# Seven products for eight in the HGRN projection of heads 2 to 7, and another order of the last normalisation

## The chip, the core and the metric

The kernel is one program on one core of a Trainium2 chip. Its engines are TensorE (PE in the profile, with its weight loads as PEld), VectorE (DVE), ScalarE (ACT), GpSimd (POOL) and SyncE (SP, which issues DMAs). Each has a queue of its own and runs it in order; they meet at semaphores. The metric is the time of one execution on the device in microseconds (us). On-chip memory is SBUF; TensorE writes to PSUM, here to two tensors: `prod_ps` (four banks of 128 x 512, for the products with weights) and `side_ps` (two pairs of banks of 128 x 1024, for everything else).

## What is computed

A hidden state of 1024 tokens with 1024 features passes a block with an HGRN2 mixer and an MLP, then a block with a convolution and retention mixer and an MLP, and is normalised once more at the end. All is float32.

```python
def _hgrn2_mixer(h, w_in, lower_bound, out_norm, w_out):
    q, f, i, g = jnp.split(h @ w_in, 4, axis=-1)
    k = (1.0 - lb) * jax.nn.sigmoid(-ff)
    qf = jax.nn.silu(q.astype(jnp.float32)) * (HGRN_HEAD_DIM ** -0.5)
    o = _hgrn2_chunk_scan(heads(qf), heads(k), heads(i.astype(jnp.float32)), heads(log_f))
    o = o * lax.rsqrt(jnp.mean(o * o, axis=-1, keepdims=True) + NORM_EPS)
    o = o.reshape(b, s, D_MODEL) * out_norm.astype(jnp.float32) * jax.nn.silu(g.astype(jnp.float32))
    return o.astype(h.dtype) @ w_out
# chunk scan, with decays from f: S_t = diag(f_t) S_{t-1} + k_t v_t^T ; o_t = S_t^T q_t, 8 heads of 128
# block 1: x = x + mix(rmsnorm(x)); x = x + squared_relu_mlp(rmsnorm(x)); rmsnorm(x). Block 2:
    h = h + hybrid_mixer(rms_norm(h, norm1_g), w_in, conv_w, conv_norm_g, ret_norm_g, w_out)
    h = h + sq_relu_mlp(rms_norm(h, norm2_g), w_up, w_down)
    return rms_norm(h, final_norm_g)
```

## The kernel before

**Units and products.** Weights come as a stream of units; one is a block of 128 output columns by 1024 inputs (`w_raw`, two slots). Each weight and each activation is split into a rounded high part and the rest (`w_hi`, `w_lo`; `operand_hi`, `operand_lo`), and a product of two such numbers takes three matmuls: high by high, high by low, low by high. So `product(u, slot, half, ...)` is 8 input tiles x 3 = 24 matmuls of 128 x 512 over one half of the tokens, and a unit has two halves. In what follows a "product" that is counted is one of these matmuls. A step named as `mid` stands behind the 12th. GpSimd splits a unit in `split_unit` (the high part at L710, the low at L714).

**The HGRN stage.** Head n has three units: v, f (which becomes the decay and the key k) and q. `hgrn_iteration(n)` stands once for each engine and holds three generations: the products of head n; the newer head n - 1, whose scores are computed in levels L0 to L6 (level L is the part of the chunk triangle at distance 2^L); and the older head n - 2, with the turning of v (`v`), the last level `L7`, the turning of k (`k`), the chunk sums (`kv`), the output (`o`) and its turning back (`back`). On TensorE these 13 side steps stand between the products, in `HG_ORDER`. They write the two pairs of `side_ps` in turn: a step waits in `pair_free` until the engine that reads the step two ahead of it has released the pair (`side_taken`). After how many products of head n each stands: v and L7 12, L0 24, k 36, L1 48, kv and L2 60, L3 84, o and L4 96, L5 120, L6 132, back 144.

For each level VectorE (`level`) multiplies the queries and keys by a decay that grows (L1932, for L1 the sigmoids in `hgrn_f`), renews the decay (L1933), and takes the scores from PSUM with a mask (L1954). From the product of VectorE, ScalarE gathers the weights for the next level on TensorE (`gather`, L2900 and L2901, tile `hgrn_mixed`). So a level needs VectorE's take of the level before and ScalarE's gather. Between levels VectorE scales the products (`group`, L1980), makes the keys (L2064, L2065), the norm factor of the older head (L1890 to L1895), its normalisation (L1900), the product of q with its sigmoid (L1990), and the states from kv (L2017, L2021). ScalarE takes v, k, o (L2925 and L2926) and back out of PSUM and makes the sigmoids (L2952, L2953 for f). Heads 4 to 7 are a loop of two heads on TensorE, VectorE and ScalarE.

**The paired form.** The in-projection of the second block, from its unit 6 on, is computed in eleven pairs of units. Over input tiles 0 to 3 the two units and the two token halves are a product of 2 x 2 blocks, for which seven block products are enough instead of eight; they need sums of weight blocks (S1 to S4, GpSimd in `split_paired`, high parts by ScalarE) and of activation blocks (T1 to T4, made once). A block product over two tiles is 2 x 3 = 6 matmuls. Input tiles 4 to 7 are computed in the plain way. ScalarE copies four partial results from PSUM to `in_c` (L3392); VectorE adds them to the banks (`got`: L1788, and L1798 for two buffers in SBUF).

**The end.** The last product's results are added to `x_res` piece by piece. Their squares are summed to the last normalisation (`end_last_sums`, L1244 on TensorE), each of three parts of the tokens gets its root, and `finals` (L2770 to L2778) multiplies on VectorE. SyncE stores.

## Time and profile before

| | us |
|---|---|
| median of three executions | 2270.77 |
| lowest, highest | 2270.21, 2271.34 |
| profiled execution, its own time | 2271.12 |
| profiled execution, span | 2269.2 |
| TensorE busy | 2256.1 (99%) |
| VectorE busy | 1637.3 (72%) |
| GpSimd busy | 1201.2 (53%) |
| ScalarE busy | 898.4 (40%) |

The span runs from the first to the last record of the profile; the execution's own time is 1.9 us more. Busy time is a sum over the whole program. In a timeline, what stands in brackets behind an instruction is how long its engine was idle ahead of it and which instruction ended that. Matmuls overlap in the records: a product of 0.39 us starts 0.23 us behind the one ahead, so their distance counts and not their length.

### The profile page before, as it was taken

Reading aid. Unit: us, or ns where it says so; the run is one execution under the profiler, and the core shown is the slowest. Engines: PE = TensorE matmul, PEld = TensorE weight load, DVE = VectorE, ACT = ScalarE, POOL = GpSimd, SP = SyncE. Lnnn points to the kernel's source line nnn. Section 1 sums busy time; section 2 is a strip of 40 time slices with the busy share of each in tenths; the row PEclk is TensorE's granted clock in tenths of the full one; section 3 lists DMA queues with packets and bytes.
Section 4 is the critical chain, followed back from the end, with each engine's and each line's share of the span. In section 5 each row is a group of like instructions: output and inputs, shape, how many; then the busy total and the mean of one; then the engine's idle time right before and its main releaser. Section 6 shows DMA issues by size and latency. Waiting matters only on the chain.

```text
span 2269.2 us, 32497 instructions
## 1 busy us (share of the span) xinstructions
PE 2256.1 (99%) x10794; PEld 1888.3 (83%) x10794; DVE 1637.3 (72%) x2305; ACT 898.4 (40%) x1467; POOL 1201.2 (53%) x1357
## 2 busy tenths in 40 slices
PE   9999999999999999999999999999999999999998
PEld 7888888888888888888888888888888888888887
DVE  7666666856778777876666777765787787778766
ACT  5233333324535434443432224322453454344433
POOL 4332323234566566656546665764556665666562
PEclk9999999999999999999999999999999999999999
DMA  4111010124264456455313111112335644554553
GB/s 158 38 29 37 29 37 28 38 75 148 93 214 148 176 185 201 145 190 186 112 56 121 66 38 40 53 56 102 121 134 182 213 148 176 185 203 146 186 196 138
DMA packets 59722, 273.82 MB, mean 121 GB/s; under 512 B 7152, under 2 KB 10352, under 8 KB 41712
## 3 DMA queue, kind: packets, MB, share of 16 engines
q1 hardware_dynamic: 59056, 270.51, 34.7%
q10 hardware_dynamic: 576, 2.13, 0.3%
q8 instruction: 54, 0.88, 0.2%
q14 instruction: 36, 0.29, 0.0%
HBM read 210.75 MB, written 61.87 MB: 120 GB/s over the span
## 4 chain that ended last, share of the span: by engine, by line
PE 94%; DVE 2%; DVEq 1%; ACT 1%; POOL 0%; DMA 0%; issue 0%; SPq 0%; ACTq 0%; POOLq 0%
PE prod_ps L959 10%; PE prod_ps L961 10%; PE prod_ps L960 10%; PE prod_ps L1225 8%; PE prod_ps L1227 8%; PE prod_ps L1226 8%; PE side_ps L1225 7%; PE side_ps L1226 7%; PE side_ps L1227 7%; PE side_ps L1100 2%; PE side_ps L1012 2%; PE prod_ps L1648 2%; PE prod_ps L1650 2%; PE prod_ps L1649 2%; PE prod_ps L1636 2%; PE prod_ps L1638 2%
## 5 line engine op out<-in xcount | busy, mean ns | idle before, releaser
L959 PE MATMUL prod_ps<-operand_hi,w_hi 128*128 128x512 f32 x984 | 393.1, 400 | 2.0 <-DVE operand_lo L1825 1.5
L961 PE MATMUL prod_ps<-operand_hi,w_lo 128*128 128x512 f32 x984 | 385.0, 391 | 0.0
L960 PE MATMUL prod_ps<-operand_lo,w_hi 128*128 128x512 f32 x984 | 383.9, 390 | 0.0
L710 POOL CAST w_hi<-w_raw 128x1024 fp32r<-128x1024 f32 x59 | 64.4, 1091 | 467.1 <-PE prod_ps L961 409.2
L755 POOL TENSOR_TENSOR w_lo<-w_raw,w_hi 128x256 fp32r<-128x256 f32 x168 | 155.6, 946 | 127.9 <-ACT w_hi L3049 127.1
L714 POOL TENSOR_TENSOR w_lo<-w_raw,w_hi 128x256 fp32r<-128x256 f32 x236 | 217.2, 951 | 4.7
L961 PEld LDWEIGHTS prod_ps<-operand_hi,w_lo 128*128 128x128 f32 x984 | 185.1, 188 | 40.1
L959 PEld LDWEIGHTS prod_ps<-operand_hi,w_hi 128*128 128x128 f32 x984 | 185.3, 188 | 38.6 <-DVE operand_lo L1825 1.9
L960 PEld LDWEIGHTS prod_ps<-operand_lo,w_hi 128*128 128x128 f32 x984 | 185.5, 188 | 36.0
L755 POOL TENSOR_TENSOR w_lo<-w_s,w_hi 128x256 fp32r<-128x256 f32 x168 | 129.1, 771 | 142.1 <-ACT w_more_hi L3057 115.9
L2257 DVE TENSOR_TENSOR x_res<-prod_ps,x_res 128x512 f32<-128x512 f32 x130 | 89.0, 685 | 96.2 <-PE prod_ps L1227 96.2
L3049 ACT ACTIVATE w_hi<-w_raw 128x512 fp32r<-128x512 f32 x114 | 70.9, 628 | 189.1 <-PE side_ps L1227 78.7
L2257 DVE TENSOR_TENSOR x_res<-side_ps,x_res 128x512 f32<-128x512 f32 x182 | 122.5, 684 | 27.4 <-PE side_ps L1227 23.3
L3053 ACT ACTIVATE w_hi<-w_s 128x512 fp32r<-128x512 f32 x114 | 72.0, 632 | 161.5 <-DVE w_s L2141 161.5
L755 POOL TENSOR_TENSOR w_s_lo<-w_s,w_more_hi 128x256 fp32r<-128x256 f32 x168 | 123.6, 756 | 0.0
L2242 DVE TENSOR_TENSOR wino_lo<-wino,wino_hi 128x1024 fp32r<-128x1024 f32 x78 | 110.3, 1426 | 11.3 <-ACT wino_hi L3120 9.2
L3057 ACT ACTIVATE w_more_hi<-w_s 128x512 fp32r<-128x512 f32 x114 | 71.9, 633 | 86.6 <-DVE w_s L2151 86.6
L1932 DVE TENSOR_TENSOR hgrn_kq<-hgrn_kq,hgrn_decay 128x1024 f32<-128x1024 f32 x48 | 59.3, 1235 | 51.2 <-PE side_ps L1100 49.6
L2900 ACT ACTIVATE hgrn_mixed<-hgrn_kq 128x256 f32<-128x256 f32 x56 | 23.8, 426 | 170.5 <-DVE hgrn_kq L1932 126.1
L755 POOL TENSOR_TENSOR w_a_lo<-w_raw,w_more_hi 128x256 fp32r<-128x256 f32 x84 | 68.4, 814 | 38.0 <-ACT w_more_hi L3060 38.0
L2141 DVE TENSOR_TENSOR w_s<-w_s,w_raw 128x256 f32<-128x256 f32 x114 | 77.3, 678 | 8.5
L3120 ACT ACTIVATE wino_hi<-wino 128x1024 fp32r<-128x1024 f32 x78 | 80.9, 1055 | 4.5 <-DVE wino L2246 2.7
(450 smaller groups left out, 6335.7 us busy)
## 6 DMA issues: line engine op xcount, KB each, us to landing
w_raw<-stream SPq DMA_DIRECT2D x202, 512.0 KB, 3.7
x_park<-x_res SPq DMA_DIRECT2D x45, 1024.0 KB, 8.2
x_res<-x_park SPq DMA_DIRECT2D x45, 1024.0 KB, 6.6
swapped<-op_park SPq DMA_DIRECT2D x39, 1024.0 KB, 5.0
op_park<-swapped SPq DMA_DIRECT2D x6, 1024.0 KB, 8.3
x_in<-x_t SPq DMA_DIRECT2D x16, 256.0 KB, 4.9
x_res<-x_t SPq DMA_DIRECT2D x8, 512.0 KB, 4.5
end_park<-x_res SPq DMA_DIRECT2D x4, 1024.0 KB, 3.9
```

What stands on the lines that cost most here:

```text
L714: low = nc.gpsimd.tensor_tensor(w_lo[:, slot, ks], w_raw[:, slot, ks], w_hi[:, slot, ks].bitcast(F32), ALU.subtract)
L755: return nc.gpsimd.tensor_tensor(dst, src, high.bitcast(F32), ALU.subtract)
L959: nc.tensor.matmul(into, w_h, a_h, start=(k == 0), stop=False)
L960: nc.tensor.matmul(into, w_h, a_l, start=False, stop=False)
L961: last = nc.tensor.matmul(into, w_l, a_h, start=False, stop=(k == KT - 1))
L1225: nc.tensor.matmul(into, w_h, a_h, start=first and kk == 0, stop=False, skip_group_check=not first)
L1226: nc.tensor.matmul(into, w_h, a_l, start=False, stop=False, skip_group_check=not first)
L1227: mm = nc.tensor.matmul(into, w_l, a_h, start=False, stop=kk == 1, skip_group_check=not first)
L2141: nc.vector.tensor_tensor(made[:, 2:4], made[:, 0:2], raw[:, 0:2], ALU.subtract).then_inc(w_sum, 1)
L2242: nc.vector.tensor_tensor(op_lo[op][:], src, op_hi[op][:].bitcast(F32), ALU.subtract).then_inc(s_ready, 1)
L2257: nc.vector.tensor_tensor(x_res[:, m, tokens(half)], src, x_res[:, m, tokens(half)], ALU.add).then_inc(down_taken, 1)
L3120: nc.scalar.activation(op_hi[op][:], src, ACT.Copy).then_inc(s_high, 1)
```

## The change

**The projection.** The head's units from unit 6 to unit 23, those of heads 2 to 7, become nine pairs. Three pairs hold two heads: v and f of the even one; its q and the odd one's v; f and q of the odd one. The class `PairedStage` holds the semaphores, buffers and banks of either paired stage, and `paired`, `got`, `in_copy`, `in_high_*` and `split_paired` take it as an argument. On TensorE `two_heads(n)` calls `paired` three times with the side steps at eight named places of each. Places and products of a pair: P2 18, c11 30, P6 36, c12 54, P7 60, c22 72, P4 78, c21 90. So in an even head the steps stand after 18 (v, L7), 30 (L0), 36 (k), 54 (L1), 60 (kv), 72 (L2), 90 (L3, o), 108 (L4), 126 (L5), 144 (L6, back), and in the odd head behind it, counted on, after 150 (v), 162 (L7), 168 (L0), 180 (k, L1), 198 (kv, L2), 216 (L3), 234 (o, L4), 252 (L5), 270 (L6, back). The three loops are written out head by head.

**Operands.** T1 to T4 are made in iteration 1: ScalarE scales tiles 0 and 1 in advance, VectorE subtracts (`in1_combine`, eight SCALAR_TENSOR_TENSOR of 128 x 512), ScalarE rounds (`in1_high`), VectorE makes the rests (`in1_low`). T4 takes the place of half 1 of tiles 0 and 1; for the gate units behind the pairs these are loaded from `x_t` again, and split again (`x_12`, `high_12`, `low_12`; TensorE waits for `b12_back` ahead of half 1 of unit 24). The input tiles stand in another order in `x_in`.

**VectorE and ScalarE.** Their queues are written in another order around the new copies and additions, as the diff shows for VectorE in full and for ScalarE in a part of the even head.

**The end.** Three of the eight finals of the second part (tiles 4 to 6) move to GpSimd, with the rms copied for it by ScalarE and the gain applied there too. The last-but-one piece of squares is summed by TensorE and no longer added on VectorE. VectorE takes the pieces in another order, and the stores of the last part's tiles 0 to 3 are issued by ScalarE.

```diff
+U_PAIRED1 = U_IN1 + 6
+IN1_PAIRS = (U_G1 - U_PAIRED1) // 2
...
+        x_in_at = (2, 3, 4, 5, 0, 1, 6, 7)
...
+            load_units(2, U_G1 + 2)
+            sp.wait_ge(in1.prod, 7 * (IN1_PAIRS - 1) + 2)
+            for m in range(2):
+                sp.dma_start(x_12[:, m], x_t[m, :, HALF:S]).then_inc(x_12_back, 16)
+            load_units(U_G1 + 2, U_OUT1)
...
+            sp.wait_ge(final_tile, KT // 2 + 2)
+            store_two(0, 1)
+            sp.wait_ge(pool_final, KT // 2 + 2)
+            store_two(4, 1)
+            sp.wait_ge(final_tile, KT // 2 + 4)
+            store_two(2, 1)
+            sp.wait_ge(pool_final, KT // 2 + 3)
+            sp.wait_ge(final_tile, KT // 2 + 5)
+            store_two(6, 1)
+            sp.wait_ge(final_tile, KT // 2 + 7)
...
+            pool.wait_ge(gained, KT + len(POOL_QUARTERS))
+            pool.wait_ge(rms_copied, 2)
+            for m in POOL_QUARTERS:
+                nc.gpsimd.tensor_tensor(x_res[:, m, NORM_TOKENS[1]], x_res[:, m, NORM_TOKENS[1]], work[:, 3, 0:QUARTER],
+                                        ALU.mult).then_inc(pool_final, 1)
...
+                if n >= HEADS1 or n < 2:
+                    mids = [turn_v_and_last_level, turn_k, kv_then_second_level, lambda: newer_level(3), None,
+                            lambda: newer_level(6)]
+                    ends = [lambda: newer_level(0), lambda: newer_level(1), None, out_then_fourth_level,
+                            lambda: newer_level(5), back]
+                elif n % 2 == 0:
+                    mids = [turn_v_and_last_level, turn_k, chunk_kv, None, lambda: newer_level(4), lambda: newer_level(5)]
+                    ends = [lambda: newer_level(0), lambda: newer_level(1), lambda: newer_level(2), third_level_then_out,
+                            None, sixth_level_then_back]
+                else:
+                    mids = [turn_v, lambda: newer_level(0), kv_then_second_level, lambda: newer_level(3), None, None]
+                    ends = [last_level, keys_then_first_level, None, out_then_fourth_level,
+                            lambda: newer_level(5), sixth_level_then_back]
+                return mids, ends
...
+            def two_heads(n):
+                steps = [hgrn_steps(n + k, k) for k in range(2)]
+                mids, ends = steps[0][0] + steps[1][0], steps[0][1] + steps[1][1]
+                for p in range(3):
+                    m0, m1, m2, m3 = mids[4 * p:4 * p + 4]
+                    e0, e1, e2, e3 = ends[4 * p:4 * p + 4]
+                    paired(in1, (3 * n - U_PAIRED1) // 2 + p,
+                           {"P2": m0, "c11": e0, "P6": m1, "c12": e1, "P7": m2, "c22": e2, "P4": m3, "c21": e3})
...
+            def paired(s, j, after):
...
+                part(1)
+                free(n_u)
+                seventh(b_u, A11, B11, True).then_inc(s.prod, 1)
+                part(3)
+                free(n_v)
+                sum_ready(1)
+                seventh(b_v, S1, T1, True).then_inc(s.prod, 1)
+                free(n_w)
+                seventh(b_w, A12, B21, True)
+                then("P2")
+                part(4)
+                plain(b_w, 0, 0, False).then_inc(s.prod, 1)
+                then("c11")
+                copied(1)
+                part(5)
+                sum_ready(2)
+                seventh(b_u, S2, T2, False).then_inc(s.prod, 1)
+                then("P6")
+                free(n_z)
+                plain(b_z, 0, 1, True)
+                part(6)
...
+                if j != s.reordered:
+                    third()
+                copied(3)
+                sum_ready(3)
+                seventh(b_u, S3, T3, False).then_inc(s.prod, 1)
+                then("P7")
+                if j != s.reordered:
+                    last_of_second()
+                else:
+                    third()
+                    pe.wait_ge(w_split, u + 1)
+                copied(4)
+                sum_ready(4)
+                seventh(b_u, A22, T4, False).then_inc(prod, 2)
+                then("P4")
+                if j == s.reordered:
+                    last_of_second()
+                plain(b_u, 1, 0, False).then_inc(prod, 2)
+                then("c21")
...
+            def end_piece_sums(n):
+                pe.wait_ge(sq_ready, 81 + n)
+                sums = last_sums(work[:, 2 * ((n + 1) % 2)], NORM_TOKENS[2].start, False, n == len(LAST_ORDER) - 1)
+                if n == len(LAST_ORDER) - 1:
+                    sums.then_inc(side_done, 1)
...
+                end_piece_sums(len(LAST_ORDER) - 2)
+                pe.wait_ge(gained, KT + len(POOL_QUARTERS))
                 turn_chunk(0)
-                end_last_sums()
+                end_piece_sums(len(LAST_ORDER) - 1)
                 turn_chunk(1)
...
+                if n == 1:
+                    in1_combine(T1, 0, 1, T1)
+                    in1_combine(T3, 2, 1, T3)
...
+                group(2)
+                if n == 1:
+                    in1_combine(T2, 2, 1, T1)
+                    dve.drain()
+                    in1_combine(T4, 2, 0, T2)
+                newer_level(3)
+                if n < 2:
+                    newer_level(4)
+                    group(3)
+                    if n == 1:
+                        in1_low(T1, 1)
+                    newer_level(5)
+                    group(4)
+                    finish_keys()
+                    if n == 1:
+                        in1_low(T2, 3)
+                    newer_level(6)
+                    second(4)
+                    if n == 1:
+                        in1_low(T3, 3)
+                    group(5)
+                    second(5)
+                    if n == 1:
+                        in1_low(T4, 4)
+                    return
                 group(3)
+                newer_level(4)
+                norm_factor(n - 1)
+                group(4)
                 newer_level(5)
+                normed(n)
+                second(4)
+                finish_keys()
+                if n == HEADS1 - 1:
+                    low_12()
+                group(5)
                 newer_level(6)
                 second(5)
...
+            def in1_combine(op, m, half, other):
+                if op == T1:
+                    dve.wait_ge(in1.scaled, 2)
+                for kk in range(2):
+                    last = nc.vector.scalar_tensor_tensor(
+                        in1.raw[op][:, kk], x_in[:, x_in_at[m + kk], tokens(half)], gain[:, G_MIX1, m + kk:m + kk + 1],
+                        in1.raw[other][:, kk], ALU.mult, ALU.subtract)
+                last.then_inc(in1.t_made, 1)
...
                 variance(1)
+                take(first + 5)
                 add(first + 4)
+                take(first + 6)
+                add(first + 5)
+                summed()
                 finals(0, range(3, 4))
-                take(first + 5)
-                add(first + 5)
-                take(first + 6)
-                finals(1, range(0, 1))
-                add(first + 6)
-                summed()
-                finals(1, range(1, 3))
                 take(first + 7)
-                finals(1, range(3, 5))
+                finals(1, range(0, 3))
                 variance(2)
-                finals(1, range(5, KT))
+                finals(1, (3, KT - 1))
                 finals(2, range(TURNED_TILES, KT))
...
+            def even_iteration(n, j):
...
+                f_sigmoids(n, 0)
+                copy_p1(in1, j + 1)
+                f_sigmoids(n, 1)
+                take_o(n)
+                copy_p5(in1, j + 1)
+                newer_gather(n, 4)
+                newer_gather(n, 5)
+                root(n, one_norm)
+                in_high_raw(in1, j + 2)
+                q_sigmoid(n, 0)
+                newer_gather(n, 6)
+                copy_u2(in1, j + 1)
+                in_high_s12(in1, j + 2)
+                q_sigmoid(n, 1)
+                take_back(n)
+                newer_gather(n, LEVELS - 1)
+                copy_u3(in1, j + 1)
...
+                    act.wait_ge(chunk_final, c + 1)
+                    act.dma_start(out_t[ks, :, tok].rearrange("k p t -> p k t"), x_res[:, ks, tok]).then_inc(stored, 16)
```

On VectorE, in an even head of the stage (`hgrn_kq_78` takes the new products, `hgrn_kq_79` is the newer head's, `in_c` are partial results), before, the takes of L5 and L6 and what lies between:

```order
L1932 TENSOR_TENSOR hgrn_kq_79<-hgrn_kq_79,hgrn_decay_86 128x2x32x16 [waits side_done]
L1933 TENSOR_TENSOR hgrn_decay_87<-hgrn_decay_86 128x32
L1954 COPY_PREDICATED hgrn_scores_81<-masks,side_ps 128x4x4x16 x2
L1980 TENSOR_TENSOR hgrn_kq_78<-prod_ps,inv_rms 128x2x2x128 [waits prod]
L2064 TENSOR_SCALAR hgrn_f<-hgrn_f,lb 128x1024 [waits gates]
L2065 TENSOR_SCALAR hgrn_kq_78<-hgrn_kq_78,lb 128x4x2x128
L1900 TENSOR_TENSOR o_keep<-o_keep,tok_rms 128x1024 [waits root_ready]
L1932 TENSOR_TENSOR hgrn_kq_79<-hgrn_kq_79,hgrn_decay_87 128x2x16x32 [waits side_done]
```

The same place now:

```order
L2082 TENSOR_TENSOR hgrn_kq_79<-hgrn_kq_79,hgrn_decay_86 128x2x32x16 [waits side_done]
L2083 TENSOR_TENSOR hgrn_decay_87<-hgrn_decay_86 128x32
L2104 COPY_PREDICATED hgrn_scores_81<-masks,side_ps 128x4x4x16 x2
L2051 TENSOR_TENSOR o_keep<-o_keep,tok_rms 128x1024 [waits root_ready]
L2144 TENSOR_TENSOR hgrn_kq_78<-hgrn_kq_78,sig 128x2x2x128 [waits q_sig]
L2159 TENSOR_SCALAR hgrn_f<-hgrn_f,lb 128x1024 [waits gates]
L2160 TENSOR_SCALAR hgrn_kq_78<-hgrn_kq_78,lb 128x4x2x128
L1948 TENSOR_TENSOR in_c_215<-in_c_215,in_c_214 128x512 [waits in1_copied]
L1938 TENSOR_TENSOR in_c_215<-prod_ps,in_c_215 128x512 [waits in1_prod]
L2133 TENSOR_TENSOR hgrn_kq_78<-in_c_215,inv_rms 128x2x2x128
L2082 TENSOR_TENSOR hgrn_kq_79<-hgrn_kq_79,hgrn_decay_87 128x2x16x32 [waits side_done]
```

Between the takes of L5 and L6 stand now the first product with the sigmoid and two additions more, and the take of L6 (L2082, `hgrn_decay_87`) follows behind them.

On TensorE, at the border of an even and the odd head (`hgrn_v_t_77` is v of head 1, which is the older one of iteration 3), this is what stands there now; before, 12 products lay between the turning of `o_keep` and that of v:

```order
L1201 MATMUL side_ps<-hgrn_kq_79,hgrn_mixed 128x128 [waits side_taken_even,level_mixed]
L1201 MATMUL side_ps<-hgrn_kq_79,hgrn_mixed 128x128 x3
L1120 MATMUL side_ps<-ident,o_keep 128x128 [waits side_taken_odd,o_normed]
L1120 MATMUL side_ps<-ident,o_keep 128x128 x7
L1340 MATMUL prod_ps<-in_t_hi,in_more_hi 128x512 [waits in1_copied]
L1341 MATMUL prod_ps<-in_t_lo,in_more_hi 128x512
L1342 MATMUL prod_ps<-in_t_hi,in_s_lo 128x512
L1340 MATMUL prod_ps<-in_t_hi,in_more_hi 128x512
L1341 MATMUL prod_ps<-in_t_lo,in_more_hi 128x512
L1342 MATMUL prod_ps<-in_t_hi,in_s_lo 128x512
L1120 MATMUL side_ps<-ident,hgrn_v_t_77 128x128 [waits evac,side_taken_even]
```

The first rows are L6 and `back`; v waits for the release of the pair that L6 wrote (`side_taken_even`), and 6 products lie between.

On ScalarE, the same even head, around the gather of L4 (form `128x32x8`). Before:

```order
L2952 ACTIVATE hgrn_f<-hgrn_kq_78 128x512 [waits evac]
L2953 ACTIVATE hgrn_kq_78<-hgrn_kq_78 128x2x2x128
L2900 ACTIVATE hgrn_mixed<-hgrn_kq_79 128x32x8 [waits level_fed]
L2901 ACTIVATE hgrn_mixed<-hgrn_kq_79 128x32x8
L2925 ACTIVATE o_sq<-side_ps 128x1024 [waits side_done]
```

Now:

```order
L3198 ACTIVATE hgrn_f<-hgrn_kq_78 128x512 [waits in1_used]
L3199 ACTIVATE hgrn_kq_78<-hgrn_kq_78 128x2x2x128
L3106 ACTIVATE in_c_213<-prod_ps 128x512 [waits in1_used,in1_prod]
L3198 ACTIVATE hgrn_f<-hgrn_kq_78 128x512 [waits evac]
L3199 ACTIVATE hgrn_kq_78<-hgrn_kq_78 128x2x2x128
L3178 ACTIVATE o_sq<-side_ps 128x1024 [waits side_done]
L3179 ACTIVATE o_keep<-side_ps 128x1024
L3106 ACTIVATE in_c_214<-prod_ps 128x512 [waits in1_used,in1_prod]
L3153 ACTIVATE hgrn_mixed<-hgrn_kq_79 128x32x8 [waits level_fed]
L3154 ACTIVATE hgrn_mixed<-hgrn_kq_79 128x32x8
```

The gather of L4 stood ahead of the taking of o; now it stands behind it and behind two copies of partial results.

## Rows read from the trace of the kernel before

**Rows 1.** The page's part 1: busy us (share of the span) and instructions of each engine.

```profile
PE 2256.1 (99%) x10794; PEld 1888.3 (83%) x10794; DVE 1637.3 (72%) x2305; ACT 898.4 (40%) x1467; POOL 1201.2 (53%) x1357
```

**Rows 2.** Waits of TensorE, the longest: waited for, us in total, times, longest.

```profile
PE side_ps L1244 <- DVEq L2767: 1.7, 1, 1.7
```

**Rows 3.** Timeline of TensorE: start, us, engine, line, operation, out<-in, count.

```profile
219.66 0.39 PE L960 MATMUL prod_ps<-operand_lo,w_hi 128*128 128x512 f32 x1
...
222.84 1.05 PE L1100 MATMUL side_ps<-hgrn_kq,hgrn_mixed 128*128 128x128 f32 x8
223.65 0.48 PE L959 MATMUL prod_ps<-operand_hi,w_hi 128*128 128x512 f32 x1
```

**Rows 4.** Window, one head: us; busy PE, PEld, DVE, ACT, POOL; PEclk, DMA, GB/s.

```profile
213.11:261.65 48.54, 48.54 (x285) 42.40 (x284) 32.40 (x51) 16.34 (x28) 13.39 (x15) 1.00 0.11 33
```

**Rows 5.** Tiles in_c, in_t of block 2: count, duration min/median/max in ns, starts.

```profile
L3392 ACT ACTIVATE in_c<-prod_ps x44: 577/598/601, 1285.8 to 1535.0; 128x512 f32<-128x512 f32 x44
L1788 DVE TENSOR_TENSOR in_c<-prod_ps,in_c x33: 677/692/693, 1292.3 to 1544.5; 128x512 f32<-128x512 f32 x33
...
L1798 DVE TENSOR_TENSOR in_c<-in_c,in_c x11: 640/1090/1235, 1301.7 to 1534.9; 128x512 f32<-128x512 f32 x11
...
L2468 DVE SCALAR_TENSOR_TENSOR in_t<-x_res,gain,in_t x8: 742/745/1491, 1244.7 to 1257.4; 128x512 f32<-128x512 f32 x8
```

**Rows 6.** Timeline of VectorE within one head, with idle time and its releaser.

```profile
220.53 1.21 DVE L1890 TENSOR_REDUCE tok_rms<-o_sq 128x8 f32<-128x1024 f32 x1
...
223.93 1.23 DVE L1932 TENSOR_TENSOR hgrn_kq<-hgrn_kq,hgrn_decay 128x1024 f32<-128x1024 f32 x1 [1.67 <-PE side_ps L1100]
...
226.29 0.69 DVE L1980 TENSOR_TENSOR hgrn_kq<-prod_ps,inv_rms 128x512 f32<-128x512 f32 x1 [0.18 <-issue]
226.90 0.81 DVE L2064 TENSOR_SCALAR hgrn_f<-hgrn_f,lb 128x1024 f32<-128x1024 f32 x1
...
228.28 1.22 DVE L1900 TENSOR_TENSOR o_keep<-o_keep,tok_rms 128x1024 f32<-128x1024 f32 x1
229.42 1.22 DVE L1932 TENSOR_TENSOR hgrn_kq<-hgrn_kq,hgrn_decay 128x1024 f32<-128x1024 f32 x1
...
231.75 1.24 DVE L1990 TENSOR_TENSOR hgrn_kq<-hgrn_kq,sig 128x512 f32<-128x512 f32 x1 [0.16 <-issue]
...
247.46 1.34 DVE L1932 TENSOR_TENSOR hgrn_kq<-hgrn_kq,hgrn_f 128x1024 f32<-128x1024 f32 x1 [3.90 <-PE side_ps L1100]
...
252.12 0.28 DVE L2017 COPY hgrn_state<-side_ps 128x128 f32<-128x128 f32 x1
...
255.14 1.23 DVE L1932 TENSOR_TENSOR hgrn_kq<-hgrn_kq,hgrn_decay 128x1024 f32<-128x1024 f32 x1 [0.21 <-issue]
```

**Rows 7.** Timeline of ScalarE in the same head, around the taking of o.

```profile
216.66 1.02 ACT L2925 ACTIVATE o_sq<-side_ps 128x1024 f32<-128x1024 f32 x1 [4.13 <-PE side_ps L1030]
...
218.81 0.42 ACT L2900 ACTIVATE hgrn_mixed<-hgrn_kq 128x256 f32<-128x256 f32 x1 [0.21 <-DVE hgrn_kq L1932]
...
220.64 0.63 ACT L2952 ACTIVATE hgrn_f<-hgrn_kq 128x512 f32<-128x512 f32 x1 [1.10 <-DVE hgrn_kq L1980]
```

**Rows 8.** Timeline in iteration 1: VectorE's take of L3, TensorE's L4.

```profile
69.26 1.22 DVE L1932 TENSOR_TENSOR hgrn_kq<-hgrn_kq,hgrn_decay 128x1024 f32<-128x1024 f32 x1 [1.74 <-PE side_ps L1100]
...
71.83 1.05 PE L1100 MATMUL side_ps<-hgrn_kq,hgrn_mixed 128*128 128x128 f32 x8
```

**Rows 9.** Windows at the program's start, columns as in rows 4.

```profile
6.00:8.00 2.00, 0.62 (x3) 0.18 (x1) 0.71 (x1) 1.21 (x3) 0.29 (x1) 1.00 0.95 327
8.00:10.00 2.00, 1.90 (x5) 1.52 (x6) 1.38 (x3) 1.68 (x4) 1.92 (x3) 0.57 1.04 382
10.00:14.00 4.00, 4.00 (x16) 3.21 (x15) 4.00 (x5) 3.38 (x7) 3.92 (x5) 0.79 1.06 388
```

**Rows 10.** Timeline of VectorE at the end: the last four finals.

```profile
2263.90 1.65 DVE L2778 SCALAR_TENSOR_TENSOR x_res<-x_res,gain,prod_ps 128x256 f32<-128x256 f32 x4
```

896 lines of the change are left out of this document (502 added, 394 removed).

## The prediction

> **What bounds the kernel now.** The page comes first. TensorE (PE) is busy for 2256.1 us of 2269.2 [rows 1], and in the list of waits its longest is 1.70 us, at the very end [rows 2]. So the time is the number of TensorE steps times their pace, and the question for each edit is how many steps go and whether the engines that feed TensorE still arrive in time.
>
> The pace comes from the timeline of TensorE. From 219.66 to 222.84 lie 14 products of 512 columns, 3.18 us, so 0.227 us each; a level step (eight short records) takes 0.81 us, and the first product behind it starts 0.3 us before the next one, some 0.09 us over the pace [rows 3]. A head with its 144 products and 13 side steps takes 48.5 us, in which VectorE is busy for 32.4 us, ScalarE for 16.3 and GpSimd for 13.4 [rows 4]. VectorE has about a third free, but not everywhere: what counts is the stretch between two side steps.
>
> **What goes.** A pair of units took 2 x 2 x 8 x 3 = 96 products. Now seven 2-tile products (42) and four 4-tile remainders (48) make 90. Nine pairs save 54 products, 54 x 0.227 = 12.3 us, all on TensorE, which never waits here: full gain if the feeds hold. Odd heads interrupt the products nine times instead of ten, three times 0.09 = 0.3 us.
>
> **What comes on the feeding engines, and where TensorE is then late.** Each pair adds four ScalarE copies out of PSUM (0.60 us), three VectorE additions (0.69) and one addition of two SBUF buffers (median 1.09) [rows 5]; GpSimd's splitting grows from two plain units to 15 short subtractions. More important is the new spacing of side steps: with L for level, the old head had L5 at product 120, L6 at 132, back at 144, and the next v at 156. In an even head of the new order L4, L5 and L6 stand at 108, 126 and 144, back right behind L6, and the v of the odd head only 6 products later. The step v writes the PSUM pair that L6 used and so waits for VectorE's release of L6. I walk the queues from one step to the other with the durations of rows.
>
> Wait at v. VectorE can take L4 when it is done, 0.8 + 0.3 us after its start. Then come, as the order shown with the change has it: take of L4 2.36 (as 223.93 to 226.29 for another level), norm factor 1.73 (220.53 to 222.26, which is 223.93 less the idle 1.67), addition 0.79 with its drain, scaling 0.61, take of L5 2.36, normalisation 1.14 (228.28 to 229.42), first sigmoid product 1.16 (1.24 for 231.75, less the usual overlap of 0.08), keys 1.38 (226.90 to 228.28), the SBUF addition 1.15, addition 0.79, scaling 0.61, L6 up to its release 2.2 (229.42 to 231.75 less the drain) [rows 5, 6]. Sum 16.3, with the start 17.4. TensorE gets from the start of L4 to v in 0.9 + 18 x 0.227 + 0.9 + 18 x 0.227 + 0.8 + 0.9 + 6 x 0.227 = 13.1. It waits 4.3 us. With every short operation at its fastest (SBUF addition 0.75, sigmoid product 0.6) it is 3.3, at their slowest 5.6.
>
> Wait at L4 of the even head. ScalarE must gather for it, but stands in line: from the end of o, the first product P1 is done after 1.7 us, then copy of P1 0.55, two f sigmoids 1.1 (0.63 each, less overlap), take of o 1.9 (216.66 to 218.60), copy of P5 0.55, gather 0.8 (218.81 to 219.54, where the idle 1.10 begins) [rows 5, 7]: 6.6, against 18 products and a restart, 4.2. It waits 2.4 us; these durations hardly vary.
>
> Wait at L3 of the even head. Before, VectorE needed 7.7 us from the take of L1 to that of L2 (247.46 to 255.14) [rows 6]; with the two new additions 1.15 + 0.79, then 1.25 for the growing multiplication and 0.8 for the gather it is 11.7 + 0.3, against 36 x 0.227 + 1.6 + 0.8 + 0.2 = 10.8. It waits 1.2 (0.7 to 1.8). Wait at L3 of the odd head: kv and L2 stand together and L3 comes 18 products later instead of 24; state updates 3.0 (252.12 to 255.14) [rows 6], 1.25, 0.8 and 0.4 of hand-offs against 5.0: 0.5.
>
> That is 8.4 us for two heads. Heads 2 to 7 hold three such periods, which don't recover between them since TensorE sets the time: 25.2 us, bounds 6.9 and 10.6 a period (the upper with 0.4 at the even head's v).
>
> Head 1 makes the operands. Eight SCALAR_TENSOR_TENSOR of 0.745 (5.3 us with overlap) [rows 5] and a drain are put ahead of VectorE's takes of L2 and L3. The slack there was the idle 1.74 ahead of VectorE's take, and 0.5 between the end of the gather (69.26 + 1.23 + 0.75 = 71.24) and the level at 71.83 [rows 8]; 5.5 - 2.2 = 3.3, and with the hand-offs 0.7 at L3 and 3.0 at L4, 3.7 us (3.3 to 4.5). The four lows behind find VectorE idle. The first pair's L0 waits 0.5 (0 to 1.8) behind ScalarE's wait for GpSimd's sums. Waits in all 29.4, bounds 24 and 38.
>
> At the shared access of VectorE and GpSimd row and rule meet. The addition of two SBUF buffers took between 0.64 and 1.235 us for one size [rows 5], and the sigmoid product 1.24 while GpSimd was at work [rows 6]. The Trainium skill (SBUF — State Buffer, "SBUF: two separate sides") says that a VectorE operation with two SBUF inputs and a GpSimd operation exclude each other for a whole instruction. It speaks against this change, which gives both more of such work. By it alone the slow durations would be the usual ones and the waits nearer to 38 than to 29; the rows show both, so I keep the middle.
>
> TensorE's clock. At the start of the program, behind an idle stretch (0.62 of 2 us busy), the granted clock was 0.57 for 2 us, near the lower of its two levels, 1.2 of 2.4 GHz, and 0.79 for the 4 us behind [rows 9], a loss of 0.86 + 0.84 = 1.7 us. Waits of 4.3 us are new in mid-kernel. I take one such loss in all; bounds 0 and three (5.1).
>
> Reload of tiles 0 and 1: it is issued behind the last pair's second product, some 80 products ahead of its use; ScalarE's two and VectorE's two operations (about 3 us) fit in the 24 products ahead of the half that needs them. Nothing. Input tiles in another place in x_in: nothing. Loops of heads 4 to 7 written out: no idle stood at their borders, so nothing.
>
> **The end.** TensorE waited 1.70 us for VectorE's sum, and the last four finals ran to 2265.55 [rows 10]. Three quarter finals (0.43 each, from the group of four) go to GpSimd, the sum of the last-but-one piece goes to TensorE, and the last sums no longer stand behind VectorE's queue. That brings the last sums and the last finals some 2 us forward. Against it stand three more gain operations on ScalarE ahead of the first spread. I take -2.0, bounds -3.0 and -0.5; the stores follow the finals and overlap.
>
> **Sum.** Against the profiled execution's own 2271.1: -12.3 - 0.3 + 29.4 + 1.7 - 2.0 = +16.5, so 2287.6; the median of the three runs is 0.3 lower, so **2287 us**. With the bounds: -15.6 + 24 = +8 (2279) to -13.1 + 38 + 5.1 = +30 (2301).
>
> **Rivals.**
> Faster: the waits are covered. This mechanism is that VectorE and ScalarE arrive in time at v and L4, which needs 4.3 and 2.4 us less in their queues than the rows give. For it speaks that the second block runs eleven such pairs and no wait of TensorE anywhere is over 1.7 us [rows 2]; against it that no level steps stand there. Price: 2271 - 12.6 - 2.0 = 2256. It decides from the point where v no longer follows L6 by less than VectorE's queue.
> Half: only the waits that the order forces (3.3 at v at most, some of L4) remain, as fast operations overlap more than I think. 12 to 19 us of waits give 2268 to 2276.
> Worse: slow VectorE operations throughout and clock losses at each long wait, above 2300.
> That the change does not do what it says can be left out: the order has 90 products in a pair.
>
> **How the numbers follow.** Forecast with its bounds (2279 to 2300) 0.70; half 0.12; covered 0.11; worse 0.07. The range of 2268 to 2300 holds 0.8. A measurement of this kernel can tell some 0.2%, 4.5 us, from no change. Faster by more: covered and a little of half, 0.13. Within: 0.05. Slower: 0.82.
>
> **What would show it.** Right: among TensorE's waits three of about 4 us ahead of v of heads 3, 5 and 7 for VectorE, three of about 2.4 us ahead of L4 for ScalarE's gather, one of 3 us in head 1 at L4; the last product of head 7 some 17 us later than before; VectorE without idle time from L4 to L6 of even heads. Wrong: no such waits, two heads in 93 us instead of 101.

## The result: slower by 1.9%

| | us |
|---|---|
| before, median of 5 | 2270.77 |
| after, median of 5 (2311.92 to 2318.8) | 2312.46 |
| after : before | 1.0189, 95% interval 1.0179 to 1.0200 |
| after, profiled execution: its time, its span | 2318.8, 2317.0 |

The change costs 41.7 us where I had forecast 16.5. The profiled execution is the slowest of the five, 6.3 us above their median. The page of the changed kernel (part 1) against [rows 1]:

```profile
PE 2265.6 (98%) x10744; PEld 1891.4 (82%) x10744; DVE 1691.0 (73%) x2351; ACT 941.5 (41%) x1553; POOL 1272.1 (55%) x1423
```

Fewer products, and yet TensorE is busy for 9.5 us longer and idle for 38 us more. The list of its waits shows where that begins (before, [rows 2] was the longest):

```profile
PE side_ps L1120 <- DVE hgrn_scores L2104: 24.7, 6, 6.3
PE side_ps L1201 <- ACT hgrn_mixed L3154: 11.8, 7, 3.1
PE side_ps L1114 <- ACT hgrn_v L3165: 1.5, 1, 1.5
```

L1120 is the turning of v, L1201 a level. The kinds of wait that I had forecast are there. In the timeline of TensorE, the iterations of heads 2 and 3:

```profile
78.31 2.08 PE L1201 MATMUL side_ps<-hgrn_kq,hgrn_mixed 128*128 128x128 f32 x8 [3.07 <-ACT hgrn_mixed L3154]
...
126.07 1.16 PE L1201 MATMUL side_ps<-hgrn_kq,hgrn_mixed 128*128 128x128 f32 x8 [0.85 <-ACT hgrn_mixed L3154]
136.74 1.16 PE L1201 MATMUL side_ps<-hgrn_kq,hgrn_mixed 128*128 128x128 f32 x8 [1.92 <-ACT hgrn_mixed L3154]
156.83 1.97 PE L1120 MATMUL side_ps<-ident,hgrn_v_t 128*128 128x128 f32 x8 [6.34 <-DVE hgrn_scores L2104]
```

What I had nearly left out is the clock. Windows of 2 us around the turning of v (columns as in rows 4, the granted clock third from the end):

```profile
150.00:152.00 2.00, 0.48 (x3) 0.05 (x1) 2.00 (x3) 0.00 (x0) 2.00 (x3) 1.00 0.00 0
152.00:154.00 2.00, 0.00 (x0) 0.00 (x0) 1.83 (x3) 0.00 (x0) 2.00 (x3) 0.62 0.00 0
154.00:156.00 2.00, 0.00 (x0) 0.00 (x0) 1.93 (x3) 1.66 (x3) 0.77 (x1) 0.50 0.00 0
156.00:158.00 2.00, 1.17 (x6) 1.17 (x7) 1.46 (x3) 1.09 (x3) 0.00 (x0) 0.50 0.00 0
158.00:160.00 2.00, 2.00 (x8) 1.71 (x7) 0.00 (x0) 1.17 (x2) 0.00 (x0) 0.50 0.00 0
160.00:162.00 2.00, 2.00 (x6) 1.53 (x5) 0.00 (x0) 0.38 (x1) 1.42 (x2) 0.50 0.00 0
162.00:164.00 2.00, 2.00 (x12) 1.76 (x11) 0.00 (x0) 0.00 (x0) 0.00 (x0) 0.82 0.03 8
```

While TensorE waits, the grant goes to 0.50, the lower of its two levels (1.2 of 2.4 GHz), and it stays there for 6 us of full work. Summed as busy time times what the grant lacks to 1, that is 2.9 us behind this wait. The stage has six such places: behind the level at 78 (2.9), v at 157 (2.9), L4 at 244 (1.6), v at 265 (1.7), v at 372 (3.0) and v at 427 (2.8), together 15.0 us.

One period of two heads, from the L0 of an odd head to the next, in the changed kernel and in the kernel before (windows):

```profile
165.54:272.69 107.15, 97.43 (x549) 83.89 (x548) 79.19 (x116) 43.87 (x80) 48.50 (x51) 0.95 0.10 30
```

```profile
189.78:286.85 97.07, 97.07 (x568) 84.80 (x567) 64.74 (x102) 32.67 (x56) 26.78 (x30) 1.00 0.11 34
```

VectorE has 14.5 us more to do in a period, ScalarE 11.2, GpSimd 21.7.

The sum over the profiled execution: 3.0 us come ahead of iteration 1 (a wait of 1.16 us at 35.5 with 3.4 us of low clock behind it; in all runs of the variants iteration 1 begins within 0.8 us of before, so I take it for scatter), 47.1 us in the HGRN and gate units, and -2.3 from there to the end. The 47.1 are -12.6 for the products, 39.3 of waits, 15.0 of clock, and 5.4 that no listed wait holds.

These 47.8 us are the profiled execution's. The difference of the medians is 41.7, and no trace shows the median execution. An estimate from the traces of e3, e4 and e6 below, which have the same stage with 2.2 to 7.3 us less of waits and lose 11.7, 11.0 and 11.3 us to the clock: in the median execution the clock costs some 11 to 12 us and not 15.

### The profile page after: what moved, and what is told of

Its sections match the earlier page's. It is cut to its first block, busy times and chain, and to the rows that moved or that the text cites. A ratio compares the mean times of both kernels' runs of the same rounds, so it can differ in the third digit from the quotient of the medians.

```text
span 2317.0 us, 32451 instructions
## 1 busy us (share of the span) xinstructions
PE 2265.6 (98%) x10744; PEld 1891.4 (82%) x10744; DVE 1691.0 (73%) x2351; ACT 941.5 (41%) x1553; POOL 1272.1 (55%) x1423
## 4 chain that ended last, share of the span: by engine, by line
PE 88%; DVE 7%; DVEq 2%; ACT 1%; issue 1%; SPq 0%; DMA 0%; POOL 0%; ACTq 0%
PE prod_ps L1475 8%; PE prod_ps L1476 8%; PE prod_ps L1477 8%; PE side_ps L1475 7%; PE side_ps L1476 7%; PE side_ps L1477 7%; PE prod_ps L1061 6%; PE prod_ps L1062 6%; PE prod_ps L1063 6%; PE prod_ps L1352 3%; PE prod_ps L1354 3%; PE prod_ps L1353 3%; PE prod_ps L1342 2%; PE prod_ps L1340 2%; PE prod_ps L1341 2%; PE side_ps L1201 2%
## 5 line engine op out<-in xcount | busy, mean ns | idle before, releaser
L1061 PE MATMUL prod_ps<-operand_hi,w_hi 128*128 128x512 f32 x696 | 276.7, 398 | 2.2 <-DVE operand_lo L1976 1.1
L1063 PE MATMUL prod_ps<-operand_hi,w_lo 128*128 128x512 f32 x696 | 272.4, 391 | 0.0
L1062 PE MATMUL prod_ps<-operand_lo,w_hi 128*128 128x512 f32 x696 | 272.3, 391 | 0.0
L849 POOL TENSOR_TENSOR w_lo<-w_raw,w_hi 128x256 fp32r<-128x256 f32 x168 | 155.2, 943 | 129.1 <-ACT w_hi L3377 128.5
L804 POOL CAST w_hi<-w_raw 128x1024 fp32r<-128x1024 f32 x41 | 45.7, 1114 | 276.2 <-PE prod_ps L1063 175.3
L808 POOL TENSOR_TENSOR w_lo<-w_raw,w_hi 128x256 fp32r<-128x256 f32 x164 | 157.9, 993 | 3.3
L1061 PEld LDWEIGHTS prod_ps<-operand_hi,w_hi 128*128 128x128 f32 x696 | 131.7, 189 | 30.9 <-DVE operand_lo L1976 1.8
L1063 PEld LDWEIGHTS prod_ps<-operand_hi,w_lo 128*128 128x128 f32 x696 | 131.5, 189 | 28.2
L1062 PEld LDWEIGHTS prod_ps<-operand_lo,w_hi 128*128 128x128 f32 x696 | 131.8, 189 | 26.0
L1352 PE MATMUL prod_ps<-operand_hi,w_hi 128*128 128x512 f32 x320 | 131.1, 410 | 0.0
L1354 PE MATMUL prod_ps<-operand_hi,w_lo 128*128 128x512 f32 x320 | 127.2, 398 | 0.0
L1353 PE MATMUL prod_ps<-operand_lo,w_hi 128*128 128x512 f32 x320 | 126.8, 396 | 0.0
L2082 DVE TENSOR_TENSOR hgrn_kq<-hgrn_kq,hgrn_decay 128x1024 f32<-128x1024 f32 x48 | 65.0, 1355 | 54.4 <-PE side_ps L1201 53.4
```

The costliest lines, as they stand in the source:

```text
L808: low = nc.gpsimd.tensor_tensor(w_lo[:, slot, ks], w_raw[:, slot, ks], w_hi[:, slot, ks].bitcast(F32), ALU.subtract)
L849: return nc.gpsimd.tensor_tensor(dst, src, high.bitcast(F32), ALU.subtract)
L1061: nc.tensor.matmul(into, w_h, a_h, start=(k == 0), stop=False)
L1062: nc.tensor.matmul(into, w_h, a_l, start=False, stop=False)
L1063: last = nc.tensor.matmul(into, w_l, a_h, start=False, stop=(k == KT - 1))
L1352: nc.tensor.matmul(into, w_h, a_h, start=first, stop=False, skip_group_check=not start)
```

## The experiments

The theory: TensorE waits for the order of the queues of VectorE and ScalarE, a long wait brings the low clock with it, and neither is a must of the seven products. If so, orders alone give the time back. All figures of runs are medians; before was run beside each and lay between 2270.0 and 2270.6.

### The end alone

The kernel before, with only the end part of the diff.

> The kernel before with only the end part of the change: three quarter finals on GpSimd, the last-but-one piece summed by TensorE, VectorE's and SyncE's new order, two stores by ScalarE. My theory: the end is worth -1.9 us by itself (in the trace of the changed kernel the start of the second MLP is 49.7 us later than before and the end of the span 47.8 us), so 2268.9 against 2270.8. Rival: the difference of 1.9 us is the scatter of the two profiled executions, and the end alone is within 0.5 us of before. A third, that the new stores cost time: over 2271.

Measured: 2269.0 against 2270.46, ratio 0.9992 (0.9983 to 1.0001). A gain of about 1.5 us, though the interval just includes no change. So the end did not cost time, and all of the loss is the projection's. The wait of [rows 2] is down to 0.34 us in this run's timeline of TensorE:

```profile
2257.71 0.58 PE L1252 MATMUL side_ps<-ones,sq_sum 128*128 128x1 f32 x4 [0.34 <-DVEq L2778]
```

### L6 first on VectorE

```diff
                 second(4)
+                newer_level(6)
                 finish_keys()
                 if n == HEADS1 - 1:
                     low_12()
                 group(5)
-                newer_level(6)
                 second(5)
```

(and ScalarE's `q_sigmoid(n, 1)` behind the gather of L7 and, in odd heads, the taking of v.)

> The changed kernel, VectorE taking L6 ahead of the keys, the reload's low parts and the last group of the head, and ScalarE's second q sigmoid moved behind the turning back and the gather of L7. Queue theory: the waits at v of heads 3, 5, 7 (6.3, 6.0, 6.3 us) fall to about 1.2 (5.1 us of VectorE's queue go behind L6) and that of iteration 8 (4.45) to under 1; with them goes most of the low clock behind each (about 3 us apiece, 12 in all); in return L0 of the odd heads waits 1 to 1.5 us. Sum -18.6 - 12 + 4 = -27, near 2286. Rival, work theory: VectorE is short of time over the whole head because GpSimd's work makes its operations slower; then the wait moves to L0 and L1 of the odd head and the total falls by less than 8 us. Second rival: the clock falls anyway, as it follows many short waits: the waits fall by 18 and the time by 18 only.

Measured: 2288.8, so -23.7 us of the 27 that I had expected. This is the decisive run: not one instruction was taken away. Its list of waits:

```profile
PE side_ps L1201 <- ACT hgrn_mixed L3154: 11.8, 7, 3.1
PE side_ps L1120 <- DVE hgrn_scores L2104: 4.6, 3, 1.7
PE side_ps L1114 <- ACT hgrn_v L3165: 3.1, 2, 1.6
```

The waits at v went from 24.7 to 4.6 us, and the clock lost 3.4 us in place of 15.0 in the stage (both by the profiled executions). L0 of the odd heads, where I expected 1 to 1.5 us, waited 0.15; the 1.63 came at L0 of iteration 8 instead. The first rival (less than 8 us) falls. The second (the waits fall by 18 and the time by 18 only, since the clock falls anyway) falls too: the waits of the stage went from 39.3 to 20.8 us, so by 18.5, but the time by 23.7, and the clock was low at two places in place of six.

### The gather of L4 first on ScalarE

```diff
                 f_sigmoids(n, 1)
+                newer_gather(n, 4)
                 take_o(n)
                 copy_p5(in1, j + 1)
-                newer_gather(n, 4)
```

> The changed kernel, with ScalarE gathering for L4 of the even head ahead of taking o and of the copy of P5. Queue theory: the waits of 1.9 us ahead of L4 go (3 x 1.9 = 5.7 us), but v of the odd head waits for VectorE's chain that starts at L4, so the chain starts 1.9 earlier against the same v and the wait at v stays as it is, 6.3; net -5.7, near 2306. Rival: the wait at v is set by VectorE's queue from far ahead of L4, and what is gained at L4 comes back at v: within 1 us of 2312.

Measured: 2306.8, -5.7 us. The three waits of 1.9 us at L4 are gone, and those at v are 6.35, 6.34 and 6.34. The two waits add up rather than cover each other: VectorE's chain to v begins with the take of L4, so a later L4 shifts both ends.

### v later

```diff
-                    mids = [turn_v, lambda: newer_level(0), kv_then_second_level, lambda: newer_level(3), None, None]
-                    ends = [last_level, keys_then_first_level, None, out_then_fourth_level,
+                    mids = [None, lambda: newer_level(0), kv_then_second_level, lambda: newer_level(3), None, None]
+                    ends = [turn_v_and_last_level, keys_then_first_level, None, out_then_fourth_level,
```

> The changed kernel, with v of the odd heads turned 12 products later, together with L7. Queue theory: TensorE has 2.7 us more of products ahead of the wait, so it is 3.6 instead of 6.3 in heads 3, 5 and 7: -8 us, and up to -3 more if the clock falls for a shorter time: 2301 to 2304. Rival: v's later turn delays ScalarE's taking of v and so L0 and k; half of the gain returns there: 2308.

Measured: 2304.4, -8.0 us, at the upper edge of what the theory gave; waits at v 3.30, 3.67 and 3.66. Twelve products ahead of a wait take 2.7 us off it on average, as counted. The rival, by which half of the gain returns at L0 and k, falls.

### A wait by itself

In the kernel before:

```diff
                     if ends[j] is not None:
                         ends[j]()
+                if static and n in PROBES:
+                    pe.wait_ge(probed, PROBES.index(n) + 1)
...
                     take_back(n, i, par)
+                if static and n in PROBES:
+                    for _ in range(3 * PROBES.index(n) + 1):
+                        nc.scalar.activation(o_sq[:], ho[:, n - 2], ACT.Copy)
+                        act.drain()
+                    act.sem_inc(probed, 1)
```

> The kernel before with two waits of TensorE and nothing else: behind the turning back of iteration 2 it waits until ScalarE has taken it and made one more copy of 128 x 1024 (into a buffer that is free), and in iteration 3 until it has made four. Expected waits about 3 and 6 us. Clock theory: each wait costs itself and, behind it, some microseconds at a granted clock near 0.5, 1.7 us for the short (as behind the 3.05 us wait of e2) and 3 for the long (as behind v of heads 3, 5, 7 in the changed kernel): 2270.5 + 9 + 4.7 = 2284. Rival: the clock falls in the changed kernel because of the many waits in a row and the heavier load, and a single wait in a full stretch leaves it at 1.00: 2279.5.

Measured: 2283.0, +12.4 us. The waits were 2.66 and 5.99 us, 8.65 together, so 3.8 us are left for the clock (4.7 by the windows of the profiled execution): a single wait in a stage that has none else brings it down. TensorE's rows and windows behind the shorter one:

```profile
136.31 0.79 PE L960 MATMUL prod_ps<-operand_hi,w_hi 128*128 128x512 f32 x1 [2.66 <-ACTq L2981]
```

```profile
134.00:136.00 2.00, 0.00 (x0) 0.00 (x0) 1.83 (x4) 1.88 (x3) 1.92 (x4) 0.93 0.00 0
136.00:138.00 2.00, 1.69 (x4) 1.40 (x5) 1.30 (x3) 0.87 (x2) 1.65 (x2) 0.50 0.00 0
138.00:140.00 2.00, 2.00 (x6) 1.52 (x6) 0.36 (x1) 0.00 (x0) 0.00 (x0) 0.50 0.58 125
140.00:142.00 2.00, 2.00 (x7) 1.51 (x6) 0.00 (x0) 0.00 (x0) 0.00 (x0) 0.50 0.35 137
```

and behind the longer one:

```profile
192.00:194.00 2.00, 0.06 (x1) 0.07 (x1) 0.00 (x0) 1.83 (x3) 0.00 (x0) 0.50 0.58 131
194.00:196.00 2.00, 2.00 (x5) 1.63 (x6) 0.69 (x1) 0.29 (x1) 0.00 (x0) 0.50 0.32 131
196.00:198.00 2.00, 2.00 (x8) 1.59 (x7) 0.00 (x0) 0.00 (x0) 0.00 (x0) 0.71 0.03 8
```

The shorter wait lost 3.1 us by the windows and the longer 1.6. I had them the other way round. In the longer one much of the low clock passed while TensorE stood still, where it costs nothing.

### The reload's low parts

```diff
-                if n == HEADS1 - 1:
-                    low_12()
                 group(5)
                 newer_level(6)
                 second(5)
+                if n == HEADS1 - 1:
+                    low_12()
```

> The changed kernel, with VectorE making the low parts of the reloaded tiles behind L6 and the last group of head 7, and not ahead of them. Theory: the 4.45 us wait at v of iteration 8 comes from this queue (VectorE waits there for ScalarE's high parts, which wait for the last pair's sixth product), so it goes, with the 2.8 us of low clock behind it: -7 us, near 2305. Rival: the wait is again that of VectorE's level queue, as in heads 3, 5 and 7, and only 1.5 us (the two operations) go: 2311.

Measured: 2310.4, -2.1 us. My theory of it falls, and the rival holds: the wait went from 4.45 to 2.17, by the two operations' 2.3 us, and the clock fell all the same. The total alone would not show it, as it lies near the scatter of the two kernels. VectorE never waited for ScalarE there. The rest is the same queue ahead of L6 as in every head.

### The operands in head 1

```diff
                 group(0)
+                if n == 1:
+                    in1_combine(T1, 0, 1, T1)
+                    in1_combine(T3, 2, 1, T3)
                 newer_level(1)
...
                     group(3)
                     if n == 1:
+                        in1_combine(T4, 2, 0, T2)
                         in1_low(T1, 1)
```

(The same lines and a drain go from their old places, and ScalarE's `take_v(n)` stands ahead of `in_high_more(in1, j)`.)

> The changed kernel, with the operands of head 1 made in the wider gaps (T1 and T3 between the takes of L0 and L1, T2 between L2 and L3, T4 between L4 and L5) and ScalarE taking v of head 2 ahead of the high parts of S3. Theory: the waits of 3.07 us at L4 and 1.49 at L0 of iteration 2 go, with about 1.7 us of low clock: -6 us, near 2306. Rival: the eight operations only wait elsewhere in head 1 (L1 or L3): within 2 us of 2312.

Measured: 2311.3, -1.1 us, which is inside the scatter, so the trace has to tell. The wait of 3.07 us at L4 is gone and L0 of iteration 2 begins 4.4 us earlier than in e6, whose head 1 is that of the changed kernel. But the 1.49 us at that L0 only fell to 1.25, since ScalarE came to v behind a q sigmoid and the high part of T4; L4 of the next head waited 2.50 in place of 1.92; and the clock fell behind an L4 at 343, where it had held in e2, e4 and e6, and for 3.4 us at the program's start. It held behind the L4 that waited 2.50:

```profile
129.50 0.71 PE L1201 MATMUL side_ps<-hgrn_kq,hgrn_mixed 128*128 128x128 f32 x4 [2.50 <-ACT hgrn_mixed L3153]
```

```profile
130.00:132.00 2.00, 2.00 (x13) 1.74 (x13) 1.31 (x2) 0.05 (x1) 0.00 (x0) 1.00 0.00 0
```

Behind waits of 1.9 to 2.5 us the grant fell in some places and held in others; on what that depends no run tells.

### All orders together

The edits of e2, e3, e4 and e7, and:

```diff
                 newer_level(1)
-                group(1)
+                late = 2 <= n < HEADS1 and n % 2 == 0
+                if not late:
+                    group(1)
                 if older:
                     states()
                 newer_level(2)
+                if late:
+                    group(1)
...
                 finish_keys()
-                if n == HEADS1 - 1:
-                    low_12()
                 group(5)
                 second(5)
+                if n == HEADS1 - 1:
+                    low_12()
```

> The changed kernel with all orders mended: those of e2, e3, e4 and e7, the reload's low parts last in head 7, and in even heads the second half of v behind VectorE's take of L2. Theory: no wait over 1 us is left in the stage and the clock stays at 1.00; what is left is the saving: 2270.5 - 12.6 - 1.5, plus the small hand-offs that e2 still shows (1.8 us in two heads, 5 in all): 2262, between 2258 and 2267. Rival, contention: VectorE's operations of 1.2 to 1.75 us instead of 0.7 to 1.2 beside GpSimd leave it no slack, so new waits of 1 to 2 us appear in each head: 2270 to 2278.

Measured: 2277.8. The theory's 2262 fell, and the rival named the place: VectorE had no slack left from L4 to L0 of the odd head, 20.5 us without a pause but one of 0.69, and TensorE waited 2.08 us at each of these L0. Ahead of that stretch VectorE sat idle:

```profile
224.67 1.23 DVE L2082 TENSOR_TENSOR hgrn_kq<-hgrn_kq,hgrn_decay 128x1024 f32<-128x1024 f32 x1 [3.04 <-PE side_ps L1201]
```

### The norm factor into the gap

```diff
                 group(3)
+                if late:
+                    norm_factor(n - 1)
                 newer_level(4)
-                norm_factor(n - 1)
+                if not late:
+                    norm_factor(n - 1)
...
                 newer_level(6)
-                finish_keys()
                 group(5)
+                finish_keys()
                 second(5)
```

(`late` is true in even heads; on ScalarE the gather of L4 and the taking of o went ahead of `f_sigmoids(n, 1)`.)

> The kernel of e8, with the even head's norm factor ahead of VectorE's take of L4 (where it sat idle for 3.0 us), ScalarE's gather of L4 and taking of o ahead of the second f sigmoids, the last group of every head ahead of the keys (so that the q sigmoid runs beside them), and in head 1 the lows of T3 and T4 behind the last product with the sigmoid. Queue theory: e8's waits of 2.08 us at L0 of the odd heads (3 times), 0.5 to 1.0 at L4 (3 times) and 1.27 at L0 of iteration 2 go, and 1.7 us of low clock with them: 2277.8 - 6.2 - 2.5 - 1.3 - 1.7 = 2266, between 2263 and 2270, so faster than before. Rival: VectorE has no time left in these heads and the waits come back at L5, L6 or L1: within 2 us of 2277.8.

Measured: 2266.3, ratio 0.9981 (0.9972 to 0.9990): faster than before by 0.2%, with the same seven products. The waits at L0 of the odd heads are 0.31, 0.32 and 0.40. Two periods of it, against 107.15 and 97.07 above:

```profile
145.73:239.74 94.01, 93.61 (x548) 81.38 (x549) 79.25 (x114) 43.97 (x81) 46.91 (x52) 1.00 0.11 35
239.74:334.19 94.45, 93.63 (x548) 81.39 (x549) 78.99 (x114) 44.12 (x81) 47.10 (x52) 1.00 0.11 34
```

Here stands the gain that the change meant: 97.07 - 94.01 = 3.1 us in a period (2.6 in the next), 18 products of 0.227 being 4.1. Of the 4.2 us by which this run is below before, some 1.5 belong to the end (e1). The busy times of the other engines are those of the changed kernel to within 0.4 us on VectorE and 2 on GpSimd, so their load was never the bound over the whole period; only the order was.

### Less of GpSimd

```diff
+                    w = 8 if j and s is in1 else P
-                    nc.gpsimd.tensor_copy(w_hi[:, 1, ks], w_raw[:, 1, ks]).then_inc(s.up_high, 1)
+                    nc.gpsimd.tensor_copy(w_hi[:, 1, ks, 0:w], w_raw[:, 1, ks, 0:w]).then_inc(s.up_high, 1)
```

(and the same for the subtractions that follow.)

> The changed kernel, with GpSimd's high and low parts of the pairs' second block of weights cut to 8 columns of 128 from the second pair on (so those weights are stale and the result of the heads is not the reference's): two of its casts and four of its subtractions a pair cost next to nothing. Nothing of VectorE's, ScalarE's or TensorE's queue is changed. Contention theory: VectorE's operations on two buffers in SBUF are longer while GpSimd works; between L4 and v some 3.3 us of GpSimd's work fall away, the keys go back from 1.09 and 1.22 us to about 0.8 each, and v's wait falls from 6.3 to about 5: -1.3 x 3, with the clock -4 to -6: 2307. Rival: the durations come from VectorE itself and stay: within 1 us of 2312.

Measured: 2307.2, -5.3 us. The waits at v are 5.07, 4.69 and 4.71 in place of 6.34, 5.96 and 6.34, and all waits of the stage 30.0 us in place of 39.3. The clock still lost 14.9 us in this trace. VectorE's keys and the addition of two SBUF buffers ahead of v, in the changed kernel:

```profile
257.31 1.09 DVE L2159 TENSOR_SCALAR hgrn_f<-hgrn_f,lb 128x1024 f32<-128x1024 f32 x1
258.33 1.22 DVE L2160 TENSOR_SCALAR hgrn_kq<-hgrn_kq,lb 128x1024 f32<-128x1024 f32 x1
259.47 1.21 DVE L1948 TENSOR_TENSOR in_c<-in_c,in_c 128x512 f32<-128x512 f32 x1
```

and in this run, where GpSimd's operations at that moment cover 8 columns in place of 128:

```profile
248.84 0.80 DVE L2160 TENSOR_SCALAR hgrn_f<-hgrn_f,lb 128x1024 f32<-128x1024 f32 x1
249.57 0.74 DVE L2161 TENSOR_SCALAR hgrn_kq<-hgrn_kq,lb 128x1024 f32<-128x1024 f32 x1
250.23 0.70 DVE L1949 TENSOR_TENSOR in_c<-in_c,in_c 128x512 f32<-128x512 f32 x1
```

The same three operations take 2.24 us in place of 3.52. The Trainium skill (SBUF — State Buffer, "SBUF: two separate sides") says that VectorE in a two-port mode or with two SBUF inputs and GpSimd take one pair of ports in turn, for a whole instruction. This trace agrees in that the three operations lose 1.3 us beside GpSimd's longer ones; that one engine is held off altogether it does not show, as the records of the two overlap, and in which mode an operation ran it does not tell.

### The first pair

> The kernel of e9, with the two waits left in head 2 taken up: there TensorE waits 0.47 us at k for VectorE's take of L7, which stands behind the lows of T3 and T4, and 2.52 us at L1, because ScalarE's gather stands behind the high parts of the next pair's weights, which wait for their DMA until 103.49. The lows go behind VectorE's take of L0 in iteration 2, and those high parts behind the gather of L1. Theory: both waits go, -3 us: 2263.3. Rival: GpSimd, which gets its sums a little later, is late for the second pair, so TensorE waits there instead: 2266.

```diff
                 newer_level(0)
                 group(0)
+                if n == 2:
+                    in1_low(T3, 3)
+                    in1_low(T4, 4)
...
-                in_high_raw(in1, j + 1)
+                if n > 2:
+                    in_high_raw(in1, j + 1)
                 copy_u2(in1, j)
                 take_k(n)
                 newer_gather(n, 1)
+                if n == 2:
+                    in_high_raw(in1, j + 1)
```

(The two lows go from head 1.)

Measured: 2268.1, slower than e9 by 1.8, though against the kernel before beside it the intervals of the two ratios overlap (0.9981 to 0.9999 here). I had moved a part without asking who waits for it. ScalarE's timeline and TensorE's:

```profile
103.42 0.60 ACT L3111 ACTIVATE in_c<-prod_ps 128x512 f32<-128x512 f32 x1 [9.17 <-DVE operand_lo L2281]
```

```profile
105.50 2.07 PE L1201 MATMUL side_ps<-hgrn_kq,hgrn_mixed 128*128 128x128 f32 x8 [3.53 <-ACT hgrn_mixed L3159]
```

The copy of U2 waits for the low part of T4, since it writes into the memory from which that low part is still made; k and the gather of L1 stand behind it.

```diff
+                if n > 2:
+                    in_high_raw(in1, j + 1)
+                    copy_u2(in1, j)
                 take_k(n)
                 newer_gather(n, 1)
+                if n == 2:
+                    copy_u2(in1, j)
+                    in_high_raw(in1, j + 1)
```

> The kernel of e11, with one thing more moved in head 2: ScalarE's copy of U2 behind its taking of k and the gather of L1. In e11 that copy waited 9.17 us for the low part of T4 (which I had moved back on VectorE), k and the gather stood behind it, and TensorE waited 3.53 us at L1. Theory: that wait goes, and 1.4 us of low clock with it: 2268.1 - 3.5 - 1.4 = 2263, between 2262 and 2265. Rival: TensorE then waits for that copy itself, ahead of S3, which stands right behind L1: within 1 us of 2268.

Measured: 2263.35, ratio 0.9971 (0.9960 to 0.9981), the fastest of all: 7.1 us below before and 49 below the changed kernel. Of the 7.1 some 1.5 are the end's, so the nine pairs give about 5.6 of the 12.6 us that their products are worth. Its clock fell at no wait of the stage. Of the rival 1.15 us came true, ahead of S3.

## Why the prediction went wrong, step by step

The kind, the sign and most places were right, the size was not: 16.5 forecast, 41.7 measured, above the upper bound of my range.

| term, us | forecast | measured, profiled execution |
|---|---|---|
| products and one restart fewer | -12.6 | -12.6 less the 5.4 below |
| waits at v of heads 3, 5, 7 | 12.9 | 18.6 |
| waits at L4 of even heads | 7.2 | 5.8 |
| waits at L3, even and odd | 5.1 | 3.0, all even |
| head 1, and L0 of the first pair | 4.2 | 4.6 |
| v of the even heads | 0 (0.4 each at most) | 1.6 |
| v of iteration 8 | 0 | 4.5 |
| three more of 0.4 to 0.6 | 0 | 1.3 |
| the clock | 1.7 | 15.0 |
| the end | -2.0 | -2.3, by itself -1.5 |

**The clock is the step that failed.** I saw in [rows 9] that idle time lowers the grant and what it costs, 1.7 us for one event, and then took one event in all, though I had forecast three waits of 4.3 us, one of 3 and three of 2.4. What the runs showed in its place: a loss at six places, 1.6 to 3.0 us each, 15.0 together. With my own waits and that price the sum would have been seven times 1.7 = 12, and the forecast 2298. The single wait in e5 shows that no crowd of waits is needed. By terms the profiled execution is 31 us over the forecast: 13.3 of clock, 9.9 of waits, 5.4 in no listed wait, 3.0 at the start.

**The wait at v** was mis-sized by its durations. VectorE's queue from the take of L4 to the release of L6 took 18.8 us (137.94 to 156.77), not 16.3: the take of L5 3.35 for 2.36, the keys 2.16 for 1.38, the take of L6 2.67 for 2.2, the SBUF addition 1.28 for 1.15. VectorE's rows of that queue:

```profile
137.94 1.23 DVE L2082 TENSOR_TENSOR hgrn_kq<-hgrn_kq,hgrn_decay 128x1024 f32<-128x1024 f32 x1 [5.41 <-PE side_ps L1201]
...
143.37 1.75 DVE L2082 TENSOR_TENSOR hgrn_kq<-hgrn_kq,hgrn_decay 128x1024 f32<-128x1024 f32 x1
145.05 0.72 DVE L2083 TENSOR_TENSOR hgrn_decay<-hgrn_decay 128x32 f32<-128x32 f32 x1
...
149.00 1.09 DVE L2159 TENSOR_SCALAR hgrn_f<-hgrn_f,lb 128x1024 f32<-128x1024 f32 x1
150.02 1.22 DVE L2160 TENSOR_SCALAR hgrn_kq<-hgrn_kq,lb 128x1024 f32<-128x1024 f32 x1
151.16 1.20 DVE L1948 TENSOR_TENSOR in_c<-in_c,in_c 128x512 f32<-128x512 f32 x1
...
154.10 1.74 DVE L2082 TENSOR_TENSOR hgrn_kq<-hgrn_kq,hgrn_decay 128x1024 f32<-128x1024 f32 x1
```

I had taken the durations from a stretch with GpSimd mostly idle [rows 4, 6], for a stage in which its work is 1.8 times as long. I had named the slow durations, and waits near 38 us in all for them, and kept the middle. The waits at v (5.96 to 6.34) passed even my slow bound of 5.6. e10 took part of GpSimd's work away and 1.3 to 1.6 us of each wait went with it; that the longer take of L6 has the same cause is not shown: in e10 GpSimd's work beside it was left as it was, and its multiplication stayed at 1.74.

**v of iteration 8** is a step that I closed too early. "(about 3 us) fit in the 24 products" looked at the products behind and not at the queue: the reload's operations stood ahead of L6 on VectorE, and v waits for L6. e6 shows that they were half of it, and that the other half was the order of every head, which I had not carried over to that border. The operations took 2.35 us, in my count 1.5.

**L3 of the odd head** did not come: no wait is listed there. **The end** was right. That the loops are written out and the tiles lie in another order cost nothing that a run shows: iteration 1 begins at 50.3 to 51.5 us in the variants, at 50.7 before.

**The rivals.** "Faster" was wrong for this order of the queues: it needed other orders, not less work. Its 2256 was not reached; the best order came to 2263.35. What it decided from, v no longer close behind L6 and its queue, is what e2 and e4 did. "Worse" is the one that came, with the chance of 0.07, and its two conditions held: clock losses at each long wait, and slow VectorE operations, if not throughout (the norm factor took 1.66 us where I had 1.73).

Open: the 5.4 us of the stage that no listed wait holds. Less the clock, iteration 1 keeps TensorE busy 1.8 us longer than before, and two periods of two heads are 1.2 and 1.4 us over the 92.9 that the sum gives (97.07 - 4.2). In e9, almost without waits, a period is still 0.7 over it (93.6). What these are no run tells.

## What to carry to other kernels

When work is taken from the engine that sets the time, walk every queue that feeds it, from one hand-over to the next, over the borders of the loop too, with durations from a stretch where the neighbours are as busy as they will be. Price a long wait of TensorE at itself plus 1.4 to 3.1 us of halved clock, as measured for those of 2.66 us and more here. A saving of 12.6 us brought 54 us of waits and low clock in the profiled execution, in a stage that had none; other orders of the queues took all but 3.5 us of that away (e12), and the time came down by 49.

## What the hardware showed

- A single wait of 2.66 us in a full stretch was followed by 6 us at a grant of 0.50, and cost 3.1 us; one of 5.99 us cost 1.6. So a shorter wait can cost more clock than a longer one.
- Over the traces of the changed kernel and e2 to e12, in this stage: all 32 waits of TensorE from 2.66 us up came with a fall to 0.50 that cost 1.4 to 3.1 us; of the 23 waits from 1.9 to 2.5 us 9 did, at 1.7 us each, and of the shorter ones none. In the changed kernel waits of 1.9 us lowered the grant at one place (244 us) and not at two others (137 and 351 us); waits of 2.50 (e7) and 2.52 (e9) left it at 1.00, one of 1.91 (e2) did not. Outside the stage a wait of 1.16 us (changed kernel, at 35.5 us) was followed by 6.8 us at 0.50. So the length of the wait does not decide alone.
- VectorE's TENSOR_SCALAR on one SBUF tensor, and not only its operations on two, went from 0.74 to 1.22 us while GpSimd worked.
